# First block of a two-block transformer kernel: counted products of the identity, read by nobody, at five places of each layer

## The reference

```python
x = layer_norm(x, ln_in_g, ln_in_b)
for l in range(2):
    proj = x @ w_in[l]            # na q,k,v | diff q,k,v | latents | 3 gates
    na_out  = neighbourhood_attention(na_q, na_k, na_v, na_rpb[l])
    df_out  = diff_attention(df_q, df_k, df_v, ...)
    mla_out = latent_attention(c_q, c_kv, k_rope, ...)
    merged  = sum(sigmoid(gate_pre[i] + b_gate[i]) * (out_i @ w_branch[l, i]))
    x = layer_norm(ALPHA * x + merged @ w_out[l], ln1_g[l], ln1_b[l])
    gu = x @ w_ffn_in[l]
    hidden = silu(gu[..., :2816]) * gu[..., 2816:]
    x = layer_norm(ALPHA * x + hidden @ w_ffn_out[l], ln2_g[l], ln2_b[l])
```

## Time and profile before

| | |
|---|---|
| Median of 3 runs | 1727.36 us (1724.08 to 1728.46) |
| Profiled execution, its own time | 1726.65 us |
| Span of its trace (first to last instruction) | 1725.4 us |
| Mean granted TensorE clock | 0.94 of 2.4 GHz |
| TensorE matmul busy | 1561.5 us, 91% of the span |
| VectorE busy | 1027.4 us, 60% |
| ScalarE busy | 753.1 us, 44% |
| Transfers | 263 MB, 152 GB/s over the span |
| First block, both layers | about 0 to 1010 us |

### The profile page before, as it was taken

The page is one execution under the profiler, slowest core; times in us unless marked ns, Lnnn a source line. Parts: engine busy times, 40 slices in busy tenths (PEclk is TensorE's granted clock), DMA queues, the critical chain, the costliest instruction groups (busy, mean ns, idle before and its releaser), DMA issues.

```text
span 1725.4 us, 18154 instructions
## 1 busy us (share of the span) xinstructions
PE 1561.5 (91%) x7205; PEld 1260.0 (73%) x7205; DVE 1027.4 (60%) x1309; ACT 753.1 (44%) x1020; POOL 66.7 (4%) x80
## 2 busy tenths in 40 slices
PE   5899899899997998999999978779999787889997
PEld 3687677788876886777788856667888575768886
DVE  4565676654565566767555557345676565257665
ACT  2454554343433555443334324234545452254553
POOL 1000100000001000000000011000000010000000
PEclk9999999999998999999999988679999896799999
DMA  8354535456545344335565726015555251145450
GB/s 299 124 174 133 186 123 188 148 162 200 183 169 192 119 148 158 126 122 164 178 195 179 256 76 219 1 50 170 180 186 191 92 203 48 49 137 180 160 200 32
DMA packets 165780, 263.06 MB, mean 152 GB/s; under 512 B 8832, under 2 KB 107008, under 8 KB 165184
## 3 DMA queue, kind: packets, MB, share of 16 engines
q1 hardware_dynamic: 164608, 254.30, 44.6%
q0 software_dynamic: 800, 6.56, 1.0%
q10 hardware_dynamic: 288, 1.05, 0.2%
HBM read 260.83 MB, written 1.05 MB: 152 GB/s over the span
## 4 chain that ended last, share of the span: by engine, by line
PE 63%; DVE 22%; ACT 10%; issue 2%; POOL 2%; DMA 1%; SPq 0%; ACTq 0%; DVEq 0%
PE ps L355 12%; PE ps L357 11%; PE ps L359 11%; DVE wlo L1289 7%; PE ps L437 7%; PE ps L439 6%; PE ps L438 6%; ACT whi L931 5%; DVE proj L1829 4%; DMA raw<-in_w_in 1%; PE ps L544 1%; PE ps L911 1%; ACT prob L1004 1%; DVE xTl L1315 1%; PE ps L564 1%
## 5 line engine op out<-in xcount | busy, mean ns | idle before, releaser
L1289 DVE TENSOR_TENSOR wlo<-raw,whi 128x2048 fp32r<-128x2048 f32 (+2 forms) x240 | 529.9, 2213 | 400.6 <-ACT whi L931 400.3
L931 ACT ACTIVATE whi<-raw 128x2048 fp32r<-128x2048 f32 (+2 forms) x240 | 443.1, 1852 | 341.2 <-PE ps L359 189.2
L355 PE MATMUL ps<-whi,xTh 128*128 128x512 f32 (+1 forms) x896 | 353.9, 401 | 15.2 <-DVE xTl L1315 9.6
L357 PE MATMUL ps<-wlo,xTh 128*128 128x512 f32 (+1 forms) x896 | 346.8, 393 | 0.0
L359 PE MATMUL ps<-whi,xTl 128*128 128x512 f32 (+1 forms) x896 | 346.6, 393 | 0.0
L437 PE MATMUL ps<-whi,xTh 128*128 128x512 f32 (+2 forms) x512 | 206.6, 403 | 14.1 <-DVE wlo L1289 7.7
L355 PEld LDWEIGHTS ps<-whi,xTh 128*128 128x128 f32 x896 | 172.8, 193 | 54.2 <-DVE xTl L1315 13.1
L359 PEld LDWEIGHTS ps<-whi,xTl 128*128 128x128 f32 x896 | 172.5, 192 | 36.1
L438 PE MATMUL ps<-wlo,xTh 128*128 128x512 f32 (+2 forms) x512 | 198.4, 388 | 0.0
L439 PE MATMUL ps<-whi,xTl 128*128 128x512 f32 (+2 forms) x512 | 198.4, 387 | 0.0
L357 PEld LDWEIGHTS ps<-wlo,xTh 128*128 128x128 f32 x896 | 173.0, 193 | 33.4
(11 more groups left out here) (174 smaller groups left out, 1580.6 us busy)
## 6 DMA issues: line engine op xcount, KB each, us to landing
raw<-in_w_in SPq DMA_DIRECT2D x120, 512.0 KB, 4.6
raw<-in_w_ffn_in SPq DMA_DIRECT2D x88, 512.0 KB, 4.8
raw<-in_w_up SPq DMA_DIRECT2D x88, 512.0 KB, 4.7
raw<-in_w_ffn_out SPq DMA_DIRECT2D x44, 512.0 KB, 4.4
raw<-in_w_down SPq DMA_DIRECT2D x44, 512.0 KB, 4.5
raw<-in_w_branch SPq DMA_DIRECT2D x24, 512.0 KB, 4.5
raw<-in_w_out SPq DMA_DIRECT2D x16, 512.0 KB, 4.3
raw<-in_w_o SPq DMA_DIRECT2D x16, 512.0 KB, 4.9
```

Of the source, the lines that this page charges most:

```text
L355: PE.matmul(o, ah, hi[:, j, b], start=first and kt == kt0, stop=False)
L357: PE.matmul(o, ah, lo[:, j, b], start=False, stop=False)
L931: AC.activation(m.whi[:, i % SPLIT, 0:w], m.raw[:, slot, 0:w], ACT.Copy).then_inc(s.w_hi, 1)
L1289: DV.tensor_tensor(m.wlo[:, i % SPLIT, 0:w], m.raw[:, slot, 0:w], m.whi[:, i % SPLIT, 0:w].bitcast(F32), ALU.subtract).then_inc(s.w_lo, 1)
```

## The change

A helper `busy(bank, times)` issues `times` matrix products on TensorE. The stationary operand is the 128x128 identity, the moving operand the same identity four times over (128 rows, 512 columns, plain float32), the destination a bank of PSUM that nobody reads before it is written again. It is called five times in each layer, with 7+7+3+3+5 = 25 products in the first layer and 3+7+3+3+5 = 21 in the second, 46 in all. To write the banks safely two waits are added or moved: `exped` of the last attention's heads ahead of the first scores (second layer only), and `pair_out`, which moves from the first product with the values to the start of the differential attention. `probs_out` now stands behind `busy` in the first round that uses it.

```diff
+    def busy(bank, times):
+        for _ in range(times):
+            PE.matmul(ps[:, bank, :].rearrange("p (r c) -> p r c", r=4), m.ident[:], spread(m.ident[:], [P, 4, P]), start=True,
+                      stop=True)
...
-        for i, (j, th, before) in enumerate(((0, 0, x_ready), (1, 0, x_ready_turn), (0, 1, x_ready), (1, 1, None))):
+        def x_ready_busy(th, kt):
+            if kt == 0:
+                busy(3, 3 if L else 7)
+            x_ready(th, kt)
+
+        for i, (j, th, before) in enumerate(((0, 0, x_ready), (1, 0, x_ready_turn), (0, 1, x_ready_busy), (1, 1, None))):
...
         fill(0, 0)
         for g in range(5):
+            if g == 0:
+                if h0:
+                    PE.wait_ge(s.exped, h0)
+                busy(3, 7)
             if g < 4:
                 score_pair(g0, h0, g)
...
             if g == 0:
+                PE.wait_ge(s.pair_out, m_na + 4)
+                busy(7, 3)
                 PE.wait_ge(s.turn_lo, latents)
...
             if g:
-                PE.wait_ge(s.probs_out, p0 + g)
-                PE.wait_ge(s.pair_out, m_na + 4)
                 if y0 + g - 1:
                     PE.wait_ge(s.heads_out, y0 + g - 1)
+                if g == 1:
+                    busy(7, 3)
+                PE.wait_ge(s.probs_out, p0 + g)
...
         end = NSTEP - 1
         up(0, before=up_turn)
+        busy(3, 5)
         h_turn()
```

## The result

| | before | changed |
|---|---|---|
| Median, same chip | 1725.91 us (8 runs) | 1730.92 us (8 runs, 1728.67 to 1732.84) |
| Ratio | | 1.0028, interval 1.0017 to 1.0039 |
| Profiled execution, span | 1725.4 us | 1729.7 us |
| Mean granted clock | 0.940 | 0.949 |
| TensorE busy | 1561.5 us | 1587.9 us |

The change makes the kernel 5.0 us slower (2.9 to 6.7 by the interval). The prediction was 1732, 5.1 us above the profiled execution of before. The clock is higher and the kernel is slower: more of TensorE's time at full speed, but 26 us more of busy time.

What follows compares the result with a forecast made beforehand. It took TensorE, busy for 91% of the span, as the bound, with waits that also lower its clock. Costs of 17.9 us less 12.8 us won gave 5.1 us slower, forecast 1732 us, range 1720 to 1741.

Steps and rivals of the forecast that it cites:

- A product's price: One 512-column plain float32 product on TensorE costs 0.865 us, twice that at 1.2 GHz.
- The half-price rival: Two records of a product together take 0.43 us; kernel 6.2 us faster, 1720.5 us; chance 8%.
- Place 1: Third `half`: almost no wait to fill, so products cost 5.75 us in the first layer and 2.2 in the second.
- Place 3: Differential attention's first scores: no wait to fill, three products cost 2.65 us in each layer, 5.3 in all.
- The rival by which places 1 and 3 are hidden: Later waits end at fixed times and absorb 13.25 us; kernel 8.2 us faster, 1718.5 us; chance 12%.
- place 2: Neighbourhood attention's first scores: seven products outlast the wait, costing 3.15 us; higher clock behind wins 5.3 us.
- place 4: First product with the values: three products end 1.5 us late, a later wait absorbs it; higher clock wins 3.4 us.
- place 5: First step of the feed-forward part: five products delay `h_turn` by 1.5 us in all; higher clock wins 4.1 us.
- slow stretches: Work behind six TensorE waits, 25.9 us nearly all at clock 0.5; at 1.0 it would take half.
- The rival that what is gained is waited away: TensorE's gain at the clock is lost at the next wait for VectorE or ScalarE: 1727 us; chance 5%.
- The net of 5.1 us: Whole kernel: costs of 17.9 us less 12.8 us won by the clock, 5.1 us slower.
- the edge at 0.3%: Smallest change a measurement of this kernel can tell from no change, 0.3% or 5.2 us; the forecast lies on it.

Runs made afterwards that it cites:

- the kernel with only these two groups: The changed kernel with only the calls of `busy` at the third `half` and ahead of the differential attention's first scores: 1736.84 us, ratio 1.0069.
- the mix: Four rounds of 4 transposes and 4 products of 64 rows, behind the second layer's `h_turn` wait, in the changed kernel with regrouped `busy` work; one execution, 1771 us.
- the kernel with two further groups: Kernel with 5, 3 and 4 products in three waits, plus products ahead of the second `half`'s weights and the third product with the values: 1715.18 us, ratio 0.9937.

## Why the prediction was right

**A product's price** was right: 0.87 us, from the scores of 96 partitions. The half-price rival is out by the records themselves. The Trainium skill ("Perfetto Trace Analysis", Engine Utilization) puts FP32_LOW_HIGH at half the output rate; a record of 512 columns takes 0.43 us here, but a plain float32 product is two of them, so the product runs at a quarter.

**Place 1** was right in mechanism and size in the first layer (5.62 us against 5.75) and priced 0.45 us too dear in the second (1.74 against 2.2). ScalarE's copy moved from 46.16 to 52.55, and the wait behind it did not shrink: 4.74 us in the kernel with only these two groups, which leaves the wait unfilled, where it was 4.52.

**Place 3** was right: 2.67 us in each layer, and nothing behind it takes them up. The rival by which places 1 and 3 are hidden is out: without them the kernel gains 11.7 us by the medians (1730.92 and 1719.27 us) and 10.7 by the two ratios, where 13.25 were expected. Point by point the two traces are 12.8 us apart over the first block (31.63 and 30.71 at the start, 1001.39 and 987.64 at its end), nearly the predicted sum; the rest is lost outside of the places.

**Places 2, 4 and 5** won what half of their slow stretches promised, in each of the six cases, to 0.3 us: 3.05 and 2.17 us behind place 2, 1.56 and 1.63 behind place 4, 1.34 and 2.51 behind place 5. The delays were a little shorter than predicted (1.41 and 1.50 us at place 2, 0.51 in both layers at place 5). Place 4's own delay was taken up by the wait of 2.60 us, of which 1.42 is left (1.1 predicted).

**The clock.** That these products hold it was right. The reason given was right only in part. The prediction took from the earlier trace rows that 64 partitions and transposes don't count and 128 partitions do. In the experiments transposes over the whole array and products of 64 and of 128 partitions all held the clock in the waits, transposes of the whole array raised it as well, and only products of 64 partitions and the mix didn't raise it. The Trainium skill ("TensorE: Matmul & The Clock Gate", Part 4) says that transposes don't count as busy in the same way; here 60 of them raised the clock and 63 held it, so this case disagrees, and the statement in the prediction that transposes would win nothing is wrong.

**No change of the sign by later waits.** The rival that what is gained is waited away did not hold at places 2, 4 and 5. It does hold elsewhere: at the second `half` and at the third product with the values, where the kernel with two further groups won nothing, and at the first step of the second block.

**What was off.** The net of 5.1 us was 4.4 at the places. That the medians are 5.0 us apart, almost to the tenth what was forecast, is partly luck: the two profiled executions are 4.3 us apart, with 0.77 us at the start and −0.8 us in the second block that no term of the sum stands for. The chance for slower (46%) and for no change (35%) came from the edge at 0.3%; the measured 0.28% lies at it, with an interval (0.17 to 0.39%) that reaches to both sides of it but not down to zero.

## What to carry to other kernels

Products that nobody reads pay only inside a wait and only for as long as it lasts: read from the timeline where TensorE idles, not where a stage begins, and divide the wait by the price of one product. Then ask of the slow stretch behind whether TensorE sets the pace there; where weights or VectorE do, a faster clock turns into the next wait. Here 24 of the 46 products in three of the five places made a kernel 0.7 to 0.8% faster than before, where all 46 made it 0.28% slower.

## What the runs showed of the hardware that was not expected

- What held the clock did not always raise it: products of 64 partitions in six waits kept it at 1.00, and 11.6 us of the same products did not bring it from 0.50 to 1.00 (one execution).
- Transposes over 128 partitions held the clock in six waits of six, and raised it from 0.50 within 4 us.
- A wait of 1.90 us brought the clock down in one layer, and one of 1.91 us in the other didn't; a wait of 2.69 us (ahead of 197.81) brought it down in the changed kernel, and 2.59 us at the same place before did not; one of 3.63 us ahead of `h_turn` did so before and did not in the kernel with only the two groups outside of waits. Its length alone doesn't decide.
- A slow stretch may be free: 20.12 us with and without one between the same two instructions.
